# A decoder trunk on one core: attention's bias laid out per query by DMA, and attention's scale and shift in two halves

## The chip, the core and the metric

The kernel runs on one core of one Trainium2 chip. The metric is the device time of one execution in microseconds (us), as the median of the runs; lower is better. The profile is that of one more execution, recorded by the hardware profiler.

## The reference

Two decoder layers on 256 tokens of width 1024, all in fp32. Layer 0 has a pooling mixer and a dense SwiGLU; layer 1 has differential attention with a bias that depends on the distance of query and key, and then a mixture of eight SwiGLU experts. Each sub-layer takes `rms_norm(x) * (1 + scale) + shift`, where scale and shift come from a conditioning vector `c`:

```python
mod_all = silu(c) @ w_mod + b_mod                    # shift, scale, gate, twice for each layer
h = rms_norm(x, norm_g[1, 0]) * (1 + scale1) + shift1
q, k, v = split(h @ w_qkv)
bias = rel_bias[rel_bucket(q_pos, k_pos)]            # depends on q_pos - k_pos alone
s = q @ k.T + bias[head]                             # for each of the 2 halves of a head
p = softmax(where(k_pos <= q_pos, s, -inf))
a = p[0] - lam * p[1]
x = x + gate1 * rms_norm((rms_norm(a @ v) * (1 - lambda_init)) @ w_o)
```

## The kernel before

All five engines run hand-ordered instruction streams that meet at semaphores. Weights come in units of 1 MB (two DMAs of 512 KB on SyncE's queue) into a ring of six, `raw`; a unit's slot is filled again when VectorE's `unit_done` says that the unit six before has been used. A weight unit is split into a high and a low part: ScalarE's `high` (L721, 1.9 us) copies it, rounded, into one of three slots of `whi`, VectorE's `low` (L1099, 2.3 us) subtracts and writes `wlo`. TensorE then does three products, high by high, low by high and high by low (`three`, L1665 to L1667). Units of `w_mod` are instead multiplied by columns of `silu(c)` on VectorE (L1111, L1113).

The change lies between the dense SwiGLU of layer 0 and attention. The order of the work there, for the two tiles `t` of 128 tokens:

- TensorE ends the down projection (tile 0, then tile 1). ScalarE squares each tile (`square_down`, L844), GpSimd makes the inverse root (L605, L607), VectorE gates it (`gated_tile`, L1161) and adds the residual (`residual_tile`, L1168). ScalarE squares the sum (`square_residual`, L849), GpSimd makes its inverse root, VectorE scales (`normalize_tile`, L1303), and TensorE turns the tile by eight transposes (L1881).
- TensorE also sums the rows of attention's scale and shift into columns: `column_sums`, L1870 and L1871, 16 products with one column, 32 records in the trace, at helper line L1683. VectorE makes `modc` of them (L1312, L1313), in its order behind `gated_tile` of tile 1 and ahead of `residual_tile` of tile 1.
- ScalarE's `modulate_tile(t, b)` scales and shifts half a turned tile, four instructions at L833, and rounds it (L836, `thi`); VectorE subtracts (`low_from`, L1103, `tlo`). ScalarE begins with this only after `square_residual(1)`. The first products of attention are the values' first half ("group 0"): tile 0 and then tile 1, each by two units of four blocks (`kh`), 12 products of 512 columns for each. Then come groups 1 to 5.

The bias: GpSimd stores a row of 384 values for each of 8 heads (L622, 12 KB, near 41 us) and reads it back with overlapping rows (L641, 1 MB, near 82 us), which gives each query its keys, but in reverse order of the queries. TensorE multiplies it by a reversed identity, four products of 512 columns in fp32 (`bias(b)`, L1874: 0 and 1 after the transposes of tile 0, 2 after those of tile 1, 3 after group 0), and ScalarE copies each result into `bias_t` (L866). VectorE's first `row_max` of attention waits for it (L1347).

## Time and profile before

| | us |
|---|---|
| median of 3 runs | 1382.52 (1381.74 to 1385.71) |
| the profiled execution | 1383.44 |
| its span in the trace | 1381.4 |

| engine | busy us | share |
|---|---|---|
| TensorE, products | 1348.3 | 98% |
| VectorE | 1163.2 | 84% |
| ScalarE | 900.8 | 65% |
| GpSimd | 76.6 | 6% |

A busy time says only that instructions were running, and TensorE's ends are modelled; what an edit is worth is read from the chain of waits at its place and from the timelines there. A product in fp32 gives two records. The granted clock of TensorE (PEclk) is 1.00 at 2.4 GHz and 0.50 at 1.2 GHz.

### The profile page before, as it was taken

What the parts mean: (1) busy time and instruction counts of PE and PEld (TensorE: products, weight loads), DVE (VectorE), ACT (ScalarE), POOL (GpSimd) and SP (SyncE); (2) the same over time, 40 slices, a digit from 0 to 9 for tenths busy, and PEclk for the clock granted to TensorE, in tenths of its full rate; (3) what the DMA queues carried; (4) which work ended last, traced back from release to release, by engine and by line L of the source; (5) the groups of instructions that cost most, each with busy time, mean ns of one, the idle gap of its engine ahead of it and who ended that gap; (6) DMA issues with size and microseconds to landing.
All of it is one profiled execution on the core that took longest, in us unless ns stands there. A gap on an engine that the chain in (4) does not pass through costs nothing.

```text
span 1381.4 us, 19455 instructions
## 1 busy us (share of the span) xinstructions
PE 1348.3 (98%) x6869; PEld 1124.0 (81%) x6869; DVE 1163.2 (84%) x944; ACT 900.8 (65%) x749; POOL 76.6 (6%) x95
## 2 busy tenths in 40 slices
PE   6999999999899999999999999999999999999996
PEld 4599999898678888888888888888888888888885
DVE  6867778788869988888888888888888888898884
ACT  3353334556657777777777777777777777777772
POOL 2610000100210000000000000000000000000000
PEclk9999999999999999999999999999999999999998
DMA  9998889688259999999999999999999999999990
GB/s 363 407 351 291 309 313 336 229 295 315 108 191 353 412 395 357 394 374 384 367 388 389 350 404 372 371 378 382 388 347 403 381 365 382 379 385 356 411 351 33
DMA packets 210074, 475.13 MB, mean 344 GB/s; under 512 B 14977, under 2 KB 38609, under 8 KB 210017
## 3 DMA queue, kind: packets, MB, share of 16 engines
q1 hardware_dynamic: 204928, 457.76, 88.6%
q0 software_dynamic: 4944, 16.35, 3.8%
q8 instruction: 35, 0.57, 0.2%
q10 hardware_dynamic: 144, 0.26, 0.0%
q14 instruction: 23, 0.18, 0.0%
HBM read 465.39 MB, written 8.93 MB: 343 GB/s over the span
## 4 chain that ended last, share of the span: by engine, by line
PE 93%; DVE 3%; ACT 1%; issue 1%; DMA 1%; POOL 0%; SPq 0%; DVEq 0%
PE ps L1665 29%; PE ps L1667 28%; PE ps L1666 28%; PE ps L2114 2%; DMA raw<-w_mod 1%; PE ps L1683 1%; DVE wlo L1443 1%; PE ps L1745 1%; PE ps L1949 0%; PE ps L2080 0%; PE ps L1649 0%; PE ps L1679 0%; DVE wlx L1443 0%; DVE hs L1392 0%; PE ps L2038 0%
## 5 line engine op out<-in xcount | busy, mean ns | idle before, releaser
L1443 DVE TENSOR_TENSOR wlx<-raw,whx 128x2048 fp32r<-128x2048 f32 x168 | 384.7, 2291 | 97.6 <-ACT whx L979 96.8
L1443 DVE TENSOR_TENSOR wlo<-raw,whi 128x2048 fp32r<-128x2048 f32 x168 | 384.0, 2287 | 4.5 <-ACT whi L979 3.0
L979 ACT ACTIVATE whi<-raw 128x2048 fp32r<-128x2048 f32 x168 | 322.3, 1920 | 88.7 <-PE ps L1667 87.0
L979 ACT ACTIVATE whx<-raw 128x2048 fp32r<-128x2048 f32 x168 | 322.3, 1919 | 83.7 <-PE ps L1667 83.7
L1665 PE MATMUL ps<-whi,thi 128*128 128x512 f32 x516 | 207.8, 403 | 1.1 <-DVE tlo L1415 0.6
L1667 PE MATMUL ps<-whi,tlo 128*128 128x512 f32 x516 | 201.6, 391 | 0.0
L1666 PE MATMUL ps<-wlo,thi 128*128 128x512 f32 x516 | 201.3, 390 | 0.0
L1665 PE MATMUL ps<-whx,thi 128*128 128x512 f32 x460 | 179.9, 391 | 0.5 <-DVE tlo L1415 0.5
L1667 PE MATMUL ps<-whx,tlo 128*128 128x512 f32 x460 | 179.2, 390 | 0.0
L1666 PE MATMUL ps<-wlx,thi 128*128 128x512 f32 x452 | 175.9, 389 | 0.0
L1665 PE MATMUL ps<-thi,whi 128*128 128x256 f32 x480 | 136.3, 284 | 2.1 <-DVE tlo L1103 2.1
L1666 PE MATMUL ps<-tlo,whi 128*128 128x256 f32 x480 | 135.8, 283 | 0.0
L1667 PE MATMUL ps<-thi,wlo 128*128 128x256 f32 x480 | 135.8, 283 | 0.0
L1099 DVE TENSOR_TENSOR wlo<-raw,whi 128x2048 fp32r<-128x2048 f32 x44 | 99.8, 2288 | 37.4 <-ACT whi L721 37.4
L1665 PE MATMUL ps<-whi,ahi 128*128 128x512 f32 x300 | 118.1, 394 | 0.6 <-DVE alo L1103 0.6
L1667 PE MATMUL ps<-whi,alo 128*128 128x512 f32 x300 | 116.8, 389 | 0.0
L1666 PE MATMUL ps<-wlo,ahi 128*128 128x512 f32 x300 | 116.8, 389 | 0.0
L1665 PEld LDWEIGHTS ps<-whi,thi 128*128 128x128 f32 x516 | 97.0, 188 | 23.4 <-issue 2.8
L1667 PEld LDWEIGHTS ps<-whi,tlo 128*128 128x128 f32 x516 | 96.8, 188 | 21.1
L1666 PEld LDWEIGHTS ps<-wlo,thi 128*128 128x128 f32 x516 | 97.1, 188 | 18.5 <-issue 0.2
L721 ACT ACTIVATE whi<-raw 128x2048 fp32r<-128x2048 f32 x44 | 83.0, 1907 | 41.0 <-PE ps L1667 41.0
L1665 PEld LDWEIGHTS ps<-whx,thi 128*128 128x128 f32 x460 | 86.4, 188 | 20.9 <-issue 3.2
(283 smaller groups left out, 1908.8 us busy)
## 6 DMA issues: line engine op xcount, KB each, us to landing
raw<-moe_w_gu SPq DMA_DIRECT2D x448, 512.0 KB, 6.2
raw<-moe_w_down SPq DMA_DIRECT2D x224, 512.0 KB, 6.4
raw<-w_mod SPq DMA_DIRECT2D x88, 512.0 KB, 5.6
raw<-ffn_w_gu SPq DMA_DIRECT2D x44, 512.0 KB, 5.3
raw<-w_qkv SPq DMA_DIRECT2D x24, 512.0 KB, 5.2
raw<-ffn_w_down SPq DMA_DIRECT2D x22, 512.0 KB, 5.0
shift_w<-w_mod SPq DMA_DIRECT2D x8, 512.0 KB, 15.7
raw<-w_o SPq DMA_DIRECT2D x8, 512.0 KB, 5.8
```

The source lines that it names most:

```text
L721: act.activation(whi[:, q % SPL, :], raw[:, r % RAW, :], ACT.Copy).then_inc(hi_ready, 1)
L979: act.activation(m_hi[m % MRING], raw[:, r % RAW, :], ACT.Copy).then_inc(hi_ready, 1)
L1099: dve.tensor_tensor(wlo[:, q % SPL, :], raw[:, r % RAW, :], whi[:, q % SPL, :].bitcast(F32), ALU.subtract).then_inc(unit_done, 1)
L1443: dve.tensor_tensor(m_lo[m % MRING], raw[:, r % RAW, :], m_hi[m % MRING].bitcast(F32), ALU.subtract).then_inc(unit_done, 1)
L1665: pe.matmul(out, a_hi, b_hi, start=start, stop=False, skip_group_check=check)
L1666: pe.matmul(out, a_hi, b_lo, start=False, stop=False, skip_group_check=check)
L1667: return pe.matmul(out, a_lo, b_hi, start=False, stop=stop, skip_group_check=check)
L1683: mm = pe.matmul(out[:, k:k + 1], rows[:, ROW[l][g], k * P:k * P + P], ones[:, 0:1], start=True, stop=True)
L1745: mm = pe.matmul(ps[:, 4 + 2 * t + g // 2, (g % 2) * FC:(g % 2) * FC + FC], pooled_t[:, 2 * g + k, t * P:t * P + P], poolw[:, g, k, :], st ...
L2114: mm = pe.transpose(ps[:, 6, jj * P:jj * P + P], actf[:, jj * P:jj * P + P], ident)
```

## The change

The 384 values of each head are stored once for each of the 128 queries, by one DMA that repeats its source (8 partitions, 128 times, 12 KB each: 1.57 MB written). It is issued by GpSimd after `f_ahi` counts 3 (third step of the dense SwiGLU) instead of near 41 us. The load goes straight into `bias_t`, with a step from query to query that is one value short of the stored row, so that the order is right; it is issued behind the last inverse root before attention. The reversed identity, its four products, ScalarE's four copies and the waits for them are gone. Scale and shift are summed in halves: `half_sums(0)`, the transposes of tile 0, then `half_sums(1)`, and four small products (`keep_clock`). `modc` follows in halves, the first ahead of `gated_tile` of tile 1, the second behind it. ScalarE modulates the first half of tile 0 ahead of `square_residual(1)`. The low part of the values' second unit is made in halves around VectorE's `normalize_tile(1)`, and the transposes of tile 1 move between the first and second half of group 0's tile 0.

```diff
-    consts[:, 4] = np.eye(P)[::-1]
...
-    bias_dram = nc.dram_tensor("bias_by_distance", (NH, S + P), F32, kind="Internal").ap()
+    bias_dram = nc.dram_tensor("bias_by_distance", (P, NH, S + P), F32, kind="Internal").ap()
...
-        bias_rev = scr[:, 4096:6144].rearrange("p (h k) -> p h k", h=NH)
...
-            pool.wait_ge(dist_ready, 2)
-            pool.dma_start(bias_dram, bias_row).then_inc(dist_stored, 16)
+            pool.dma_start(numbers[:, 0:3], consts_in[:, 4 * P:4 * P + 3]).then_inc(wr_loaded, 16)
+
             inverse_roots(0, 2)
             inverse_roots(1, 0)
...
             next_gain(3, (0, 2))
-            pool.dma_start(consts[:, 2:5, :], consts_in[:, 2 * P:5 * P].rearrange("p (i s) -> p i s", i=3)).then_inc(more_consts_loaded, 16)
-
+            pool.dma_start(consts[:, 2:4, :], consts_in[:, 2 * P:4 * P].rearrange("p (i s) -> p i s", i=2)).then_inc(more_consts_loaded, 16)
+
+
+            pool.wait_ge(dist_ready, 2)
+            pool.wait_ge(f_ahi, 3)
+            pool.dma_start(bias_dram.rearrange("q h k -> h q k"),
+                           bias_row.unsqueeze(1).broadcast_to([NH, P, S + P])).then_inc(dist_stored, 16)
             pool.wait_ge(dist_stored, 16)
-            pool.wait_ge(lam_prod, 2)
-            pool.dma_start(bias_rev, bass.AP(tensor=bias_dram.tensor, offset=0,
-                                             ap=[(1, P), (S + P, NH), (1, S)])).then_inc(bias_loaded, 16)
             next_gain(5, (0, 5))
             inverse_roots(1, 2)
             inverse_roots(2, 0)
+
+            pool.dma_start(bias_t, bass.AP(tensor=bias_dram.tensor, offset=P - 1,
+                                           ap=[(NH * (S + P) - 1, P), (S + P, NH), (1, S)])).then_inc(bias_loaded, 16)
 
...
@@ -853,17 +853,15 @@
             square_residual(0)
             square_down(1)
             high(R_QKV + 1, Q_QKV + 1)
+            act.wait_ge(col_ready, 7)
+            modulate_tile(0, 0)
             square_residual(1)
-            act.wait_ge(col_ready, 7)
-            for t in range(T):
-                for b in range(2):
-                    modulate_tile(t, b)
+            act.wait_ge(col_ready, 9)
+            modulate_tile(0, 1)
+            modulate_tile(1, 0)
+            modulate_tile(1, 1)
             act.wait_ge(ss_ready, 4 * 2 + T)
             high(R_GROUP[1], Q_QKV + 2)
-
-            def copy_bias(b):
-                act.wait_ge(bias_ps, b + 1)
-                act.copy(bias_t[:, 2 * b:2 * b + 2, :], bank(b).rearrange("p (h k) -> p h k", h=2)).then_inc(bias_ready, 1)
 
             def qkv_out(g):
                 act.wait_ge(unit_used, Q_QKV + 2 * g + 2)
@@ -875,11 +873,8 @@
                     dst = vs[:, :, (c - 4) * 512:(c - 3) * 512]
                 act.copy(dst, src).then_inc(qkv_ready, 1)
 
-            for b in range(3):
-                copy_bias(b)
             high(R_GROUP[1] + 1, Q_QKV + 3)
             qkv_out(0)
-            copy_bias(3)
             for g in range(2, 6):
                 high(R_GROUP[g], Q_QKV + 2 * g)
                 high(R_GROUP[g] + 1, Q_QKV + 2 * g + 1)
@@ -1306,20 +1301,37 @@
...
             gated_tile(0, 5, 0, Y1[0])
             residual_tile(0, T, Y1[0])
             normalize_tile(0)
+
+            def attention_columns(h):
+
+                a, b = slice(4 * h, 4 * h + 4), 3 - h
+                dve.wait_ge(col_ps, 6 + h)
+                dve.scalar_tensor_tensor(modc[:, 0, a], ps[:, b, 0:4], 1.0, cols[:, 8, a], ALU.add, ALU.mult).then_inc(col_ready, 1)
+                dve.tensor_copy(modc[:, 1, a], ps[:, b, 4:8]).then_inc(col_ready, 1)
+
+            attention_columns(0)
             gated_tile(0, 5, 1, Y1[1])
-
-            dve.wait_ge(col_ps, 7)
-            dve.scalar_tensor_tensor(modc[:, 0, :], ps[:, 3, 0:KC], 1.0, cols[:, 8, :], ALU.add, ALU.mult).then_inc(col_ready, 1)
-            dve.tensor_copy(modc[:, 1, :], ps[:, 3, KC:2 * KC]).then_inc(col_ready, 1)
+            attention_columns(1)
             residual_tile(1, T, Y1[1])
+
+            def low_tile(t, b):
+                dve.wait_ge(ht_hi, 4 + 2 * t + b + 1)
+                part = (slice(None), slice(4 * b, 4 * b + 4), slice(t * P, t * P + P))
+                low_from(tlo3[part], hv3[part], thi3[part], ht_lo)
+
+            def low_half(h, sem_out):
+
+                a, sl = slice(h * D, h * D + D), (Q_QKV + 1) % SPL
+                dve.wait_ge(hi_ready, Q_QKV + 2)
+                dve.tensor_tensor(wlo[:, sl, a], raw[:, (R_QKV + 1) % RAW, a], whi[:, sl, a].bitcast(F32), ALU.subtract).then_inc(sem_out, 1)
+
+            low_tile(0, 0)
+            low_half(0, values_lo)
             normalize_tile(1)
-            for t in range(T):
-                for b in range(2):
-                    dve.wait_ge(ht_hi, 4 + 2 * t + b + 1)
-                    part = (slice(None), slice(4 * b, 4 * b + 4), slice(t * P, t * P + P))
-                    low_from(tlo3[part], hv3[part], thi3[part], ht_lo)
-                    if t == 0 and b == 0:
-                        low(R_QKV + 1, Q_QKV + 1)
+            low_tile(0, 1)
+            low_half(1, unit_done)
+            low_tile(1, 0)
+            low_tile(1, 1)
             n = N_QKV_MODS
             for g in range(6):
                 if g:
...
                 dve.wait_ge(sc_ps, h + 1)
                 if h == 0:
-                    dve.wait_ge(bias_ready, 4)
+                    dve.wait_ge(bias_loaded, 16)
...
             down_tile(1, last_hi, last_lo, Q_LAST_DOWN % SPL, True).then_inc(unit_used, 1)
 
             pe.wait_ge(row_done, done_rank(0, 5))
-            column_sums(1, 1, ps[:, 3, 0:KC])
-            column_sums(1, 0, ps[:, 3, KC:2 * KC])
-
-            def bias(b):
-                pe.matmul(bank(b), reverse, bias_rev[:, 2 * b:2 * b + 2, :].rearrange("p h k -> p (h k)"),
-                          start=True, stop=True).then_inc(bias_ps, 1)
+            def half_sums(h):
+
+                for i, g in enumerate((1, 0)):
+                    for k in range(4):
+                        mm = pe.matmul(ps[:, 3 - h, 4 * i + k:4 * i + k + 1], rows[:, ROW[1][g], (4 * h + k) * P:(4 * h + k) * P + P],
+                                       ones[:, 0:1], start=True, stop=True)
+                mm.then_inc(col_ps, 1)
+
+            half_sums(0)
 
             def turn_normalized(t):
                 pe.wait_ge(h_ready, 2 * T + t + 1)
@@ -1881,13 +1896,11 @@
                         mm = pe.transpose(ps[:, 4 + 2 * t + b, (k % 4) * P:(k % 4) * P + P], hs[:, t, k * P:k * P + P], ident)
                     mm.then_inc(ht_ps, 1)
 
-            pe.wait_ge(bias_loaded, 16)
             pe.wait_ge(more_consts_loaded, 16)
             turn_normalized(0)
-            bias(0)
-            bias(1)
-            turn_normalized(1)
-            bias(2)
+            half_sums(1)
+            pe.wait_ge(col_ready, 7)
+            keep_clock(3, 4)
 
             def qkv_group(g):
 
@@ -1908,22 +1921,25 @@
 
             for t in range(T):
                 for kh in range(2):
+                    if t == 0 and kh == 0:
+                        pe.wait_ge(unit_done, R_GROUP[0] + 1)
+                    elif t == 0:
+
+                        turn_normalized(1)
+                        pe.wait_ge(values_lo, 1)
                     pe.wait_ge(ht_lo, 4 + 2 * t + kh + 1)
-                    if t == 0:
-                        pe.wait_ge(unit_done, R_GROUP[0] + kh + 1)
                     q = Q_QKV + kh
                     for kk in range(4):
                         k, w = 4 * kh + kk, slice(kk * 512, kk * 512 + 512)
+                        if t == 0 and k == 6:
+                            pe.wait_ge(unit_done, R_GROUP[0] + 2)
                         mm = three(bank(4 + t), thi3[:, k, t * P:t * P + P], tlo3[:, k, t * P:t * P + P],
                                    whi[:, q % SPL, w], wlo[:, q % SPL, w], k == 0, k == KC - 1, False)
                     if t:
                         mm.then_inc(unit_used, 1)
-            pe.wait_ge(col_ready, 7)
-            bias(3)
             for g in range(1, 5):
                 qkv_group(g)
             pe.wait_ge(qkv_ready, 4)
-            pe.wait_ge(bias_ready, 4)
```

## Rows read from the trace of the kernel before

**Rows 1.** The page's first line: span of the profiled execution.

```profile
span 1381.4 us, 19455 instructions
```

**Rows 2.** What TensorE waited for, all the run; columns: us in total, times, longest.

```profile
PE ps L1881 <- DVE hs L1303: 0.3, 1, 0.3
```

**Rows 3.** The chain that ended last, in order of time, 265 to 287 us; columns: start, us, what.

```profile
265.21 3.65 PE ps L1683 x32
...
272.49 0.76 DVE hs L1303
...
273.30 1.09 PE ps L1881 x8
...
274.39 0.86 PE ps L1874 x2
...
275.25 0.23 PE ps L1665
...
286.15 0.86 PE ps L1874 x2
```

**Rows 4.** Timeline of TensorE (PE), 262 to 276 us; columns: start, us, engine, line, operation.

```profile
268.70 1.95 PE L1881 MATMUL ps<-consts,hs 128*128 128x128 f32 x8
...
270.44 2.54 PE L1874 MATMUL ps<-scr,consts 128*128 128x512 f32 x4
```

**Rows 5.** Timeline of ScalarE (ACT), 240 to 345 us.

```profile
266.26 1.90 ACT L721 ACTIVATE whi<-raw 128x2048 fp32r<-128x2048 f32 x1
...
270.34 1.06 ACT L849 ACTIVATE ysb<-xs 128x1024 f32<-128x1024 f32 x1 [2.19 <-DVE xs L1168]
...
271.40 1.48 ACT L833 ACTIVATE tmp<-ps,modc 128x128 f32<-128x128 f32 x4
...
272.91 0.63 ACT L836 ACTIVATE thi<-tmp 128x512 fp32r<-128x512 f32 x1
```

**Rows 6.** Timeline of VectorE (DVE), 240 to 345 us.

```profile
266.48 1.22 DVE L1161 TENSOR_TENSOR ysb<-ps,rows 128x1024 f32<-128x1024 f32 x1
...
269.04 1.28 DVE L1168 SCALAR_TENSOR_TENSOR xs<-ysb,rstd,xs 128x1024 f32<-128x1024 f32 x1
...
273.58 0.69 DVE L1103 TENSOR_TENSOR tlo<-tmp,thi 128x512 fp32r<-128x512 f32 x1 [0.34 <-ACT thi L836]
...
281.55 2.30 DVE L1099 TENSOR_TENSOR wlo<-raw,whi 128x2048 fp32r<-128x2048 f32 x1 [1.11 <-ACT whi L721]
```

**Rows 7.** Windows: each engine's busy time, granted TensorE clock (PEclk), DMA share, GB/s.

```profile
67.00:68.00 1.00, 1.00 (x11) 1.00 (x9) 0.96 (x3) 0.61 (x1) 1.00 (x2) 0.50 1.09 386
...
264.00:268.00 4.00, 4.00 (x34) 3.80 (x32) 1.88 (x2) 3.57 (x5) 1.58 (x4) 1.00 0.04 11
...
268.00:272.00 4.00, 4.00 (x18) 3.15 (x18) 1.43 (x3) 1.81 (x5) 0.34 (x2) 0.57 0.00 0
```

**Rows 8.** Timeline of TensorE, small operations near 19 and 65 us.

```profile
19.35 3.57 PE L1683 MATMUL ps<-consts,rows 128*128 128x1 f32 x16 [0.96 <-DVE rows L1184]
...
64.92 1.94 PE L1784 MATMUL ps<-consts,rows 1*128 1x1 f32 x16
...
66.79 0.91 PE L1679 MATMUL ps<-zeros 128*128 128x128 bf16 x8
```

**Rows 9.** Timelines of SyncE's queue, 60 to 150 us, and of ACT, 80 to 160 us.

```profile
114.94 3.12 SPq L453 DMA_DIRECT2D raw<-ffn_w_gu  x4
...
127.66 3.70 ACT L721 ACTIVATE whi<-raw 128x2048 fp32r<-128x2048 f32 x2
```

**Rows 10.** DMA issues of the whole run: KB each, us from issue to landing.

```profile
raw<-ffn_w_gu SPq DMA_DIRECT2D x44, 512.0 KB, 5.3
...
scr<-bias_by_distance POOLq DMA_DIRECT2D x1, 1024.0 KB, 9.3
...
bias_by_distance<-scr POOLq DMA_DIRECT2D x1, 12.0 KB, 5.4
```

**Rows 11.** DMA queues between 70 and 100 us: packets, MB, share of 16 engines.

```profile
q0 software_dynamic: 576, 1.79, 15.0%
```

More of the change, by code:

```diff
@@ L120, in shape_constants @@
 def shape_constants():
-    consts = np.zeros((P, 5, P), np.float32)
+    consts = np.zeros((P, 4, P), np.float32)
     consts[:, 0] = np.eye(P)
@@ L149, in shape_constants @@
     numbers = np.arange(1, 3 * P + 1, dtype=np.float32).reshape(3, P).T
-    return np.concatenate([consts.reshape(P, 5 * P), numbers], axis=1), pool.reshape(P, -1), onehot
+    return np.concatenate([consts.reshape(P, 4 * P), numbers], axis=1), pool.reshape(P, -1), onehot
 def build_trunk(nc, x, c, w_mod, b_mod, norm_g, pool_w, pool_scale, w_qkv, w_o, subln_g, lambda_vecs,
@@ L187, in build_trunk @@
         tmp = sb("tmp", [P, 2304])
-        consts = sb("consts", [P, 5, P])
+        consts = sb("consts", [P, 4, P])
         subln = sb("subln", [P, 4])
@@ L212, in build_trunk @@
         modc = sb("modc", [P, 5, KC])
-        ident, ones, before, slots, reverse = (consts[:, i, :] for i in range(5))
+        ident, ones, before, slots = (consts[:, i, :] for i in range(4))
         thi3 = thi[:, :].rearrange("p (k s) -> p k s", k=KC)
@@ L371, in build_trunk @@
         bias_loaded = sem("bias_loaded")
-        bias_ps = sem("bias_ps")
-        bias_ready = sem("bias_ready")
         lam_prod = sem("lam_prod")
@@ L383, in build_trunk @@
         qkv_ready = sem("qkv_ready")
+        values_lo = sem("values_lo")
         sc_ps = sem("sc_ps")
@@ L618, in _ @@
             pool.dma_start(wr[:, :, :], w_router[0].rearrange("(k p) e -> p k e", p=P)).then_inc(wr_loaded, 16)
-            pool.dma_start(numbers[:, 0:3], consts_in[:, 5 * P:5 * P + 3]).then_inc(wr_loaded, 16)
-            pool.wait_ge(dist_ready, 2)
-            pool.dma_start(bias_dram, bias_row).then_inc(dist_stored, 16)
+            pool.dma_start(numbers[:, 0:3], consts_in[:, 4 * P:4 * P + 3]).then_inc(wr_loaded, 16)
             inverse_roots(0, 2)
```

## The prediction

> **What bounds the kernel now.** I read the page first, for the span [rows 1] and TensorE's 98% share, then what TensorE waited for. In the stretch that the change touches that list holds one entry, 0.3 us for the normalized tile 1 [rows 2]. So TensorE is never out of work for long there, and the question is which of its work between the down projection and attention's group 1 can go, and who is late once it has gone. The chain in order of time shows this: column sums from 265.21, then a piece through VectorE, ScalarE and GpSimd to `normalize_tile(1)` at 272.49, transposes at 273.30, `bias(2)` at 274.39, group 0 from 275.25 to 286.15 and `bias(3)` for 0.86 us [rows 3]. Group 1 starts at 287.01, and from there TensorE is solid for 45 us. My number is the new start of group 1, as what lies behind it moves with it: ScalarE, VectorE and the ring of weights are paced by TensorE there.
>
> **What goes.** Of the four bias products, 0 and 1 take 2.54 us at the low clock [rows 4]; but the chain at that time runs through the other engines to tile 1, so they fill a gap and are worth nothing by themselves. `bias(2)` and `bias(3)` are on the chain, 0.86 us each, 1.72 us together [rows 3]. ScalarE's four copies lie in waits for TensorE and are worth nothing. Group 0 must also no longer wait for the transposes of tile 1: it needs half a tile 0 alone.
>
> **The floor.** TensorE needs in any case 3.79 us of column sums (the 3.65 of the chain and its lead), 1.09 us for each set of transposes at the high clock, and 286.15 - 275.25 = 10.90 us for group 0 [rows 3]. From 265.05 that makes 265.05 + 3.79 + 2.18 + 10.90 = 281.9, and with a few tenths of small products some 282.3: at most 4.7 us could be gained. The rest of the working is why I expect little of it.
>
> **The new order, step by step.** A half of the sums is 16 records, half of 3.79, so 1.9 us: `half_sums(0)` runs from 265.05 to 266.95. VectorE, done with `normalize_tile(0)` at 266.5, waits for it and makes half of `modc` by 267.2; `gated_tile` of tile 1, 1.22 us, moves from 266.48 to 267.2 [rows 6], which nobody misses, because its residual has to wait anyway. The transposes of tile 0 follow from 267.0 to 268.1. ScalarE is free at 268.16, behind `high` [rows 5], and modulates the first quarter at once: 1.48 + 0.63 us, done at 270.3, where before it was done at 273.5.
>
> Then comes the new wait. VectorE's second half of `modc` waits for `half_sums(1)`, and queued behind it on VectorE stand the residual of tile 1, the low part that group 0 waits for, and everything after. At the high clock `half_sums(1)` ends at 270.0. At the low one 16 such records took 3.57 us near 19 us, against 1.9 [rows 8] (that stretch is shown with PEclk 1.00, but its products are twice as long as later ones, so I read it as the low clock). It then ends at 271.65. Which of the two? The granted clock was 1.00 from 264 to 268 and 0.57 from 268 to 272, behind 32 records of one column [rows 7]: the low level, 1.2 GHz, for most of that stretch. Near 64.9 us eight transposes and 16 narrow products (L1784) did not prevent a fall either: 0.50 at 67 to 68 [rows 7, 8]. The new order has just that mix there, so I take the fall, and 271.65. The Trainium skill ("TensorE: Matmul & The Clock Gate", HAM clock gate) says that the default state is throttled and activity releases the throttle. By that rule alone the new order, which puts less work on TensorE before group 0, has its first products at half speed; the trace agrees as far as the low clock at 268 to 272 goes.
>
> From 271.7 on: second half of `modc` 0.2 us, residual 1.28 [rows 6], to 273.1; low part 0.69 [rows 6], to 273.8. Group 0 then starts at 273.8, against 275.25: 1.45 us earlier. Its first 12 products take 10.90 / 4 = 2.73 us at the high clock and twice that at the low; I take three at the low clock, 0.6 us more, and end at 277.1. The transposes of tile 1 come now, 1.09 us, to 278.2. They need `normalize_tile(1)`: square of the residual at 273.15, and from there to the scaling 272.49 - 270.34 = 2.15 us as before [rows 3, 5], so 275.3 to 276.0, in time. Second half 278.2 to 280.9: its low weights come by halves, half of 2.30 us each [rows 6], the second at about 278.4, for the seventh product at 279.6, in time. Tile 1: ScalarE can modulate from 277.7, 2.1 us, and VectorE 0.69, so 280.5 and 282.6 for its two halves, against 280.9 and 283.6, in time. Group 0 ends at 286.35. Group 1 needs its low weights: `high` 281.9 to 283.8 and `low` 2.30 us to 286.15 [rows 5, 6], 0.2 us before they are wanted. **Sum:** 287.01 - 286.35 = 0.65 us. With the fall of the clock behind `half_sums(1)` instead of ahead of it, group 0 starts at 272.35, its first 12 products lose 1.3 us to the low clock, and the same addition gives 285.7, a gain of 1.3. I take the middle, **0.9 us**.
>
> **The DMAs.** Both are moved past work on GpSimd's queue. The load into `bias_t`, 1 MB, 9.3 us to land next to other traffic [rows 10], is issued near 275.5 and wanted after 330. The DMA share was 0.04 and 0.00 just before [rows 7], and the next unit is wanted by ScalarE 15 us later, so it costs nothing; without this cover it would be 2.7 us of all engines. It stands behind the last inverse root on GpSimd, and the next thing there is in attention. The store is new in kind. By the load's queue, 1.79 MB took 15.0% of 16 engines for 30 us, 72 engine-us [rows 11]; 1.57 MB are then 63, so 4 us on all 16 engines and 8 on 8. It is issued near 127.8. A weight unit issued at 114.94 lands 5.3 us later [rows 9, 10] and is read by the second `high` of the pair at 127.66, at 129.5: 9 us in hand. So I price it at nothing, with the ends: nothing (the old 1 MB load near 82 us also goes, without a gain, as TensorE didn't wait there), and the rival below. The 12 KB store took 5.4 us [rows 10], which is nearly all latency; 128 times that, 690 us, would be the far end and would block GpSimd past 256 us, where a gain is due. I don't believe it, since 0.5 to 32 KB all took about as long. One DMA that repeats a source has no row here.
>
> The rule that speaks against the store is in the Trainium skill ("DMA: Bandwidth & Descriptors", Rules for kernel authors): an outermost dimension below 16 confines a DMA to at most that many engines; here that is 8, heads being outermost. "SBUF — State Buffer" (Door 1) adds that four partitions share a port, at about 27 GB/s. By both, an estimate for 1.57 MB from 8 partitions is 29 us. No run here shows either yet.
>
> **Rivals.**
> 1. The clock stays up (`half_sums(1)` at 1.9 us and group 0 at full speed): group 0 starts at 272.35, and by the same steps group 1 at 284.4. Gain 2.6 us, 1379.9. For it: the clock is back at 1.00 right after 272; against it, the two falls above. 20%.
> 2. The low clock lasts through the whole first half of group 0: 12 products at twice 2.73 us, so 1.8 us beyond the forecast's 0.6, and group 1 at 288.2. That is the new wait on VectorE at its worst: a loss of 1.1 us, 1383.6. 12%.
> 3. The store starves the dense SwiGLU, **slower than before**. It decides once the engines that carry it are held for over 9 us. If they are held 16.6 us (half the 8 engines, or half the rate), the weights come 16.6 - 9.2 = 7.4 us late, less the 0.9 gained: 1389.0. For it: 8 source partitions only. Against it: other transfers keep their turns between its packets. 8%.
> 4. The floor: all waits vanish, and 4.7 us are gained, 1377.9. 5%.
> 5. The change doesn't do what it says, for one thing because group 1's low weights, 0.2 us in hand above, set its start again. This gives 1382 to 1383 and lies inside the forecast.
>
> **The numbers.** The profiled execution took 1383.44, its span 1381.4, so 2.0 us lie around it; it ran 0.9 above the median. The sum gives a span of 1380.5 and an execution of 1382.5; on the median's footing 1382.52 - 0.9 = 1381.6. The forecast, 0.3 to 1.6 us gained, has 55%. The range takes in rivals 1 and 2 and half a us of spread on each side: 1379.4 to 1384.2, with rivals 3 and 4 left out. 0.3% is 4.1 us, about what a measurement of this kernel can tell from no change: only rival 4 is faster by that, 5%; rival 3 slower, 8%; the rest is the same, 87%.
>
> **What would show it.** In the changed kernel: `half_sums(1)` at about 3.5 us with a granted clock of 0.5; group 0 starting some 1.5 us earlier counted from the first column sum, its first products 0.43 us apart at first; group 1 0.3 to 1.6 us earlier; no wait of TensorE for weights between 128 and 180 us; the store landing before 170 us. The prediction is wrong if TensorE waits in the dense SwiGLU, if group 1 starts over 2 us earlier or later than now, or if attention or the experts take another time than before.

## The result

The changed kernel is slower: median 1400.53 us of 4 runs (1397.42 to 1401.94), beside 1384.12 us (1381.74 to 1386.69) for the kernel before in 4 runs. The ratio is 1.0115, with an interval of 1.0099 to 1.0132. The forecast was 1381.6 in a range up to 1384.2, so the time lies 16 us above the top of the range, on the side that had 8%.

The profiled execution took 1400.59 us. The page of the changed kernel begins as follows; the span line answers to [rows 1], and the third line names what stands in the chain that ended last.

```profile
span 1398.7 us, 19447 instructions
...
PE 91%; DVE 4%; DMA 3%; ACT 1%; issue 1%; SPq 0%; DVEq 0%; POOL 0%; ACTq 0%
PE ps L1677 28%; PE ps L1679 27%; PE ps L1678 27%; DMA raw<-ffn_w_gu 2%; PE ps L2130 2%; PE ps L1768 1%; DMA raw<-w_mod 1%; PE ps L1757 1%; DVE wlo L1094 0%; PE ps L1965 0%; DVE wlo L1455 0%; PE ps L2096 0%; ACT whi L721 0%; PE ps L1695 0%; PE ps L1691 0%
```

The span grew by 17.3 us. The entry to look at is `raw<-ffn_w_gu`: 2% of 1399 us, a load of weights of the dense SwiGLU on the chain. What TensorE waited for between 100 and 340 us says it directly (us in total, times, longest):

```profile
PE ps L1677 <- DVE wlo L1094: 13.9, 2, 13.5
PE ps L1677 <- DVE tlo L1098: 2.0, 1, 2.0
```

Before, this list held one entry of 0.3 us in the same stretch [rows 2]. The second line is the start of attention's group 0, to which I come below. For the first, the chain in order of time leads back to its source, 140 to 172 us:

```profile
142.12 0.84 SPq L450
142.96 0.04 issue
143.00 26.45 DMA raw<-ffn_w_gu
169.45 0.02 issue
169.48 1.92 ACT whi L721
171.40 0.02 issue
171.42 2.31 DVE wlo L1094
```

A load of 512 KB, half a unit, was on its way for 26.45 us; such loads took 5.3 us before [rows 10]. The timelines of GpSimd, ScalarE and TensorE give the order of events: the store is issued, ScalarE waits for weights, TensorE runs out and then starts again with slow products.

```profile
129.81 1.13 POOL L637 DMA_DIRECT2D bias_by_distance<-scr  x1 [46.47 <-ACT ahi L813]
...
166.76 1.91 ACT L721 ACTIVATE whi<-raw 128x2048 fp32r<-128x2048 f32 x1 [18.88 <-DMA raw<-ffn_w_gu]
...
171.05 0.58 PE L1677 MATMUL ps<-thi,whi 128*128 128x256 f32 x1 [13.54 <-DVE wlo L1094]
```

And the DMA issues of the stretch, the view of [rows 10]: KB each, median us from issue to landing.

```profile
raw<-ffn_w_gu SPq DMA_DIRECT2D x4, 512.0 KB, 25.9
raw<-w_mod SPq DMA_DIRECT2D x4, 512.0 KB, 7.8
bias_by_distance<-scr POOLq DMA_DIRECT2D x1, 1536.0 KB, 35.2
```

The store, issued at 129.8, lands at 165.0. Within 1.8 us of it ScalarE has its unit, and 6.0 us after it TensorE works again. The windows of the changed kernel show the same as a rate (columns: stretch, sum, busy us of PE, PEld, DVE, ACT and POOL with their counts, PEclk, DMA share, GB/s):

```profile
140.00:148.00 8.00, 8.00 (x67) 7.92 (x66) 6.01 (x7) 3.04 (x3) 0.00 (x0) 1.00 0.68 106
148.00:156.00 8.00, 8.00 (x53) 7.28 (x52) 2.21 (x1) 0.00 (x0) 0.00 (x0) 1.00 0.50 58
156.00:164.00 8.00, 1.51 (x7) 0.93 (x5) 0.00 (x0) 0.00 (x0) 0.00 (x0) 0.80 0.60 91
164.00:172.00 8.00, 0.95 (x4) 0.95 (x5) 2.87 (x2) 4.30 (x3) 0.00 (x0) 0.50 0.99 371
```

In the kernel before, the last three of these stretches were

```profile
148.00:156.00 8.00, 8.00 (x48) 7.04 (x46) 6.22 (x4) 2.26 (x2) 0.00 (x0) 1.00 0.77 247
156.00:164.00 8.00, 8.00 (x68) 8.00 (x67) 6.01 (x7) 3.52 (x4) 0.00 (x0) 1.00 1.01 358
164.00:172.00 8.00, 8.00 (x51) 7.23 (x50) 6.32 (x3) 3.23 (x2) 0.00 (x0) 1.00 0.77 252
```

A DMA share of 0.50 beside 58 GB/s is the sign to learn: half of the DMA engines' time is taken, and what they move is about a quarter of what they moved before (58 beside 247 GB/s, then 91 beside 358). Much time and few bytes means that each byte takes long. Why it does is what the experiments ask.

**Where the 17.3 us went.** Up to the first column sum, my landmark, the distance grew by 282.31 - 265.05 = 17.26 us, and behind it the rest of the span is 1116.39 against 1116.35. So all of it lies ahead. 13.54 us are the wait. Behind it the first 16 products come 0.21 us apart and not 0.12 (PEclk is 0.50 until 174), which costs 1.5 us. A second wait of 0.40 us stands at 184.67. 1.35 us lie ahead of the dense SwiGLU, whose first product starts at 76.89 and not 75.54. Together this is 16.8; half a us is spread too thinly to be named. The 1.35 us are not the change's: kernels with the same code up to there differ by more. The kernel before starts it at 75.54, and at 77.10 with small products added far behind; the four kernels below whose store reads 128 partitions start it between 73.59 and 76.93.

### The profile page after: what moved, and what is told of

Read it like the earlier page. It is cut to its first block, busy times and chain, and to the rows that moved or that the text cites. A ratio compares the mean times of both kernels' runs of the same rounds, so it can differ in the third digit from the quotient of the medians.

```text
span 1398.7 us, 19447 instructions
## 1 busy us (share of the span) xinstructions
PE 1350.6 (97%) x6865; PEld 1126.9 (81%) x6865; DVE 1163.5 (83%) x947; ACT 899.5 (64%) x745; POOL 79.3 (6%) x95
## 4 chain that ended last, share of the span: by engine, by line
PE 91%; DVE 4%; DMA 3%; ACT 1%; issue 1%; SPq 0%; DVEq 0%; POOL 0%; ACTq 0%
PE ps L1677 28%; PE ps L1679 27%; PE ps L1678 27%; DMA raw<-ffn_w_gu 2%; PE ps L2130 2%; PE ps L1768 1%; DMA raw<-w_mod 1%; PE ps L1757 1%; DVE wlo L1094 0%; PE ps L1965 0%; DVE wlo L1455 0%; PE ps L2096 0%; ACT whi L721 0%; PE ps L1695 0%; PE ps L1691 0%
## 5 line engine op out<-in xcount | busy, mean ns | idle before, releaser
L1677 PE MATMUL ps<-thi,whi 128*128 128x256 f32 x480 | 136.8, 285 | 15.6 <-DVE wlo L1094 13.5
L1677 PEld LDWEIGHTS ps<-thi,whi 128*128 128x128 f32 x480 | 92.8, 193 | 16.6 <-DVE wlo L1094 14.0
```

Of the source, the lines that this page charges most:

```text
L1677: pe.matmul(out, a_hi, b_hi, start=start, stop=False, skip_group_check=check)
```

## Experiments

A landing time is from issue to landing, and "group 1" is the time from the first column sum to the second product of attention's group 1 (the first is stretched in some traces). It is 21.92 us before and 21.05 in the changed kernel. The kernel before was timed beside each set of runs.

### One copy in place of 128

The bias is stored once, as before; the load has a step of +1, so that the 128 rows of a head come in reverse order (this kernel's bias, and so its output, is that of reversed queries). All else is the changed kernel.

```diff
-            pool.dma_start(bias_dram.rearrange("q h k -> h q k"),
-                           bias_row.unsqueeze(1).broadcast_to([NH, P, S + P])).then_inc(dist_stored, 16)
+            pool.dma_start(bias_dram, bias_row).then_inc(dist_stored, 16)
...
-            pool.dma_start(bias_t, bass.AP(tensor=bias_dram.tensor, offset=P - 1,
-                                           ap=[(NH * (S + P) - 1, P), (S + P, NH), (1, S)])).then_inc(bias_loaded, 16)
+            pool.dma_start(bias_t, bass.AP(tensor=bias_dram.tensor, offset=0,
+                                           ap=[(1, P), (S + P, NH), (1, S)])).then_inc(bias_loaded, 16)
```

> The changed kernel with the bias stored once (12 KB) at the same place instead of 128 times, and loaded with a step of one value, so that the queries of the bias come in reverse order: the output differs for that reason alone, the sizes of the load are the same. Theory A: TensorE has no wait for weights in the dense SwiGLU, and what is left is the gain of the columns and of the bias products: 0.5 to 1.5 us faster than the kernel before, with 20.9 us from the first column sum to group 1, as in the changed kernel, against 22.0 before. Rival B: it stays 10 us or more slower than before.

Measured: 1384.34 us against 1384.62, ratio 1.000 (0.9988 to 1.0012). The store landed in 3.8 us, and TensorE had no wait between 100 and 260 us. Group 1 came after 20.87 us. So the loss is the size or the shape of the store, and not the place of the step, the new order in attention, or the load. The gain of 0.5 to 1.5 us that I expected can't be seen in this ratio, nor does its interval rule it out.

### The store alone, in the kernel before

```diff
+    copies_dram = nc.dram_tensor("bias_copies", (P, NH, S + P), F32, kind="Internal").ap()
...
+            pool.wait_ge(bias_loaded, 16)
+            pool.wait_ge(f_ahi, 3)
+            pool.dma_start(copies_dram.rearrange("q h k -> h q k"),
+                           bias_row.unsqueeze(1).broadcast_to([NH, P, S + P])).then_inc(dist_stored, 16)
+            pool.wait_ge(dist_stored, 32)
             next_gain(5, (0, 5))
```

> The kernel before, with one addition: the 128-fold store of 1.57 MB from partitions 0 to 7, into a DRAM tensor that nobody reads, issued by GpSimd once the third step of the dense SwiGLU is through, as in the changed kernel. Theory A (the store alone makes the loss): it lands after about 35 us, TensorE waits some 13 us for low weights near 170 us, and the time is 14 to 17 us above the kernel before. Rival B (the store is slow, but the loss needs the rest of the change): within 3 us of the kernel before.

Measured: 1400.63 us against 1383.45, ratio 1.0126 (1.0103 to 1.0148). Its DMA issues and the waits of TensorE between 100 and 340 us:

```profile
bias_copies<-scr POOLq DMA_DIRECT2D x1, 1536.0 KB, 35.1
...
PE ps L1671 <- DVE wlo L1105: 13.8, 2, 13.4
```

The same landing, the same wait, the same loss (17.2 us, at the edge of the 14 to 17 expected). This one DMA, which nobody reads, makes the kernel before as slow as the changed one. The pair is complete: without the store the loss is gone, and with the store alone it is there.

### Which property of the store costs it

The bytes, 1.57 MB, stay; what changes is which partitions they are read from. In the first kernel the product that looks the bias up writes it to all 128 partitions (its table of 8 columns is repeated 16 times by the DMA that loads it), and the store reads partitions 0, 9, 18 and so on to 63, 8 of them as before, 128 times each. In the second it reads partitions 0 to 15, 64 times each.

```diff
-            pool.dma_start(relb, rel_bias).then_inc(small_loaded, 16)
+            pool.dma_start(relb.rearrange("b (r h) -> b r h", h=NH),
+                           rel_bias.unsqueeze(1).broadcast_to([N_BUCKETS, P // NH, NH])).then_inc(small_loaded, 16)
...
+            pool.dma_start(bass.AP(tensor=bias_dram.tensor, offset=0,
+                                   ap=[(S + P, 8), (8 * (S + P), 128), (1, S + P)]),
+                           bias_row[0:64:9, :].unsqueeze(1).broadcast_to([8, 128, S + P])).then_inc(dist_stored, 16)
```

> The changed kernel, the same store of 8 rows, 128 times each, but with the row of head h taken from partition 9h (0, 9, ..., 63) instead of partition h. For that the rows are made on all 128 partitions by the same product, with the table's 8 columns repeated 16 times. Theory P (the source's partitions share few ports, two for partitions 0 to 7, eight here): the store lands in 10 to 15 us instead of 35, and the time falls by 12 us or more. Theory E (8 engines carry it, because the outermost dimension is 8, and each is slow by itself): 35 us as before and 1400 us.

```diff
+            pool.dma_start(bass.AP(tensor=bias_dram.tensor, offset=0,
+                                   ap=[(S + P, 16), (16 * (S + P), 64), (1, S + P)]),
+                           bias_row[0:16, :].unsqueeze(1).broadcast_to([16, 64, S + P])).then_inc(dist_stored, 16)
```

> The changed kernel with the store's source on 16 partitions (0 to 15), 64 times each, so an outermost dimension of 16. Theory P (four ports): the store lands after about 20 us. Theory E (16 engines instead of 8): about 20 us as well. Both expect most of the wait of TensorE in the dense SwiGLU gone, 0 to 5 us left of 13.5; read with the run that keeps 8 rows on spread partitions it tells ports from engines.

A third reads all 128 partitions, 8 times each. Here ScalarE repeats the table on the chip, so that the start of the kernel isn't held up:

```diff
+            act.copy(relb_wide.rearrange("b (r h) -> b r h", h=NH),
+                     relb.unsqueeze(1).broadcast_to([N_BUCKETS, P // NH, NH])).then_inc(relb_spread, 1)
...
+            pool.dma_start(bass.AP(tensor=bias_dram.tensor, offset=0,
+                                   ap=[(S + P, 128), (128 * (S + P), 8), (1, S + P)]),
+                           bias_row[0:128, :].unsqueeze(1).broadcast_to([128, 8, S + P])).then_inc(dist_stored, 16)
```

> The changed kernel with the store's source on all 128 partitions, 8 times each: the rows are made for 16 copies of the heads by one product, whose table ScalarE widens by a copy. Theory P (the ports of the source's partitions set the rate; 2 ports took 35.2 us, 4 took 18.5, 8 took 12.3): 16 ports leave only the engines' own time, so it lands in 7 to 10 us, no wait of TensorE for weights. Theory E (only the number of engines counts): with 16 engines like the source of 16 partitions, 18 us. Time: the kernel before less 0 to 1.5 us.

The DMA queues of the changed kernel, 130 to 166 us, and its store; then those of the 8 partitions nine apart, 130 to 150 us (packets, MB, share of 16 engines):

```profile
q0 software_dynamic: 704, 1.58, 43.2%
q1 hardware_dynamic: 1846, 2.63, 22.1%
```

```profile
q1 hardware_dynamic: 2858, 4.81, 69.1%
q0 software_dynamic: 704, 1.58, 22.7%
...
bias_by_distance<-scr POOLq DMA_DIRECT2D x1, 1536.0 KB, 12.3
```

Both stores have 8 source partitions, 704 packets and 1.58 MB in these windows. The first holds engines for 0.432 x 16 x 36 = 249 engine-us, the second for 0.227 x 16 x 20 = 73. Meanwhile the queue of weights moves 2.63 MB in 36 us in the one and 4.81 MB in 20 us in the other. The others by the same sum:

| source partitions | lands in us | engine-us | wait of TensorE for weights, us |
|---|---|---|---|
| 8 side by side (changed kernel) | 35.2 | 249 | 13.5 |
| 16 side by side | 18.5 | 0.577 x 16 x 25 = 231 | 1.6 |
| 8, nine apart | 12.3 | 73 | none |
| 128 | 11.9 | 0.194 x 16 x 22 = 68 | none |

So the number of source partitions isn't it (8 give 73 or 249), nor the bytes, nor the destination, which is the same in that pair. With 8 or 16 partitions side by side, the time per byte on an engine is 3 to 4 times as long as in the other two rows. The store from 16 lands sooner than that from 8 at nearly the same engine-us: on average it holds 231 / 18.5 = 12.5 engines at once, against 249 / 35.2 = 7.1. Both the partitions and the outermost dimension were doubled, so this step doesn't tell which of the two helped. The two stores from 8 partitions do: they differ only in how far apart the partitions lie.

The packets of the weights were hardly slower themselves: 0.221 x 16 x 36 = 127 engine-us for 2.63 MB, 48 for each MB, against 0.691 x 16 x 20 = 221 for 4.81 MB, 46 for each, next to the store from partitions nine apart. The weights were late because of the time between their packets, which fits engines that are busy with the store. Which of the 16 engines the store held stays open.

The Trainium skill ("SBUF — State Buffer", Door 1) says that four neighbouring partitions share a port and gives some 27 GB/s for each. By that, the four stores read through 2, 4, 8 and 16 ports, at 54, 108, 216 and 435 GB/s, and with the 5.4 us of the small store [rows 10] for the rest they should land in 34.5, 20.0, 12.7 and 9.0 us, an estimate. The traces agree for the first three: 35.2, 18.5 and 12.3. The fourth took 11.9 us here, with 6.57 MB of weights in the same 22 us, more than this estimate and than the 7 to 10 us expected; in the three later kernels with the same store it took 10.5, 7.9 and 7.8. Its sister rule, at most 8 engines for an outermost dimension of 8 ("DMA: Bandwidth & Descriptors", Rules for kernel authors), is not what makes the difference of the pair: the stores from 8 partitions nine apart and from 8 neighbours are alike in it.

Two of these kernels have a single time each: 1387.8 us (nine apart) and 1388.41 us (16). Their repeated table landed late, and TensorE started some 3.5 us later, with `[3.76 <-DMA scr<-onehot_in]` in its timeline at 14.55; that is this experiment's way of preparing the table, and no verdict on the store. The kernel with 128 source partitions has no such wait: 1383.58 us against 1383.45, ratio 1.0004 (0.999 to 1.0018). The change as it stands, with its source spread over the partitions, costs nothing and brings nothing that can be measured.

The same can be had without SBUF as a source. The row is stored once, early, and a second DMA makes the 128 copies from DRAM to DRAM, queries outermost:

```diff
+            pool.wait_ge(dist_ready, 2)
+            pool.dma_start(bias_once, bias_row).then_inc(dist_stored, 16)
...
+            pool.wait_ge(f_ahi, 3)
+            pool.dma_start(bias_dram, bias_once.unsqueeze(0).broadcast_to([P, NH, S + P])).then_inc(dist_stored, 16)
+            pool.wait_ge(dist_stored, 32)
```

> The changed kernel, but the 12 KB row is stored to DRAM early, as in the kernel before, and the 128 copies are made by one DMA from DRAM to DRAM, queries outermost, so no SBUF port is read. Theory P (the source's SBUF ports made the 35 us): it lands in 7 to 13 us, TensorE does not wait for weights, and the time is that of the kernel before within 2 us. Rival W (the 1.57 MB of writes to DRAM, in pieces of 1.5 KB, are slow in themselves): 20 us or more.

Measured: the copies landed in 9.1 us and held 0.289 x 16 x 15 = 69 engine-us; no wait for weights. Its single time is 1381.07 us; its dense SwiGLU began at 73.52, 2.0 us earlier than before, so this one time proves no gain. But it speaks against slow writes to DRAM as the cause: the same bytes were written here.

### The order of attention, and its clock

My forecast let the clock fall ahead of group 0, and rival 1 let it stay up. First the order alone, on top of the store from 128 partitions: the residual of tile 1 goes ahead of the second half of the columns on VectorE, so that it waits for no product.

```diff
             gated_tile(0, 5, 1, Y1[1])
-            attention_columns(1)
             residual_tile(1, T, Y1[1])
+            attention_columns(1)
```

> As the run with the source on 128 partitions, and on VectorE the residual of tile 1 stands ahead of the second half of modc, so that it doesn't wait for the second half of the column sums. If that wait is what holds up group 0, group 0 starts 0.6 to 1.3 us earlier, counted from the first column sum (about 5.7 to 6.3 us instead of 6.7 to 7.0), and group 1 0.3 to 1.2 us earlier (19.7 to 20.6 instead of 20.8 to 20.9). If ScalarE's modulation sets it, group 0 starts at the same time and nothing moves. The whole time may move by less than can be told.

Measured: 1385.11 us against 1383.45, ratio 1.0013 (1.0002 to 1.0024), so no gain, and if anything 0.1% lost. Its group 0 starts 6.04 us after the first column sum (7.1 with the store from 128 partitions alone), but group 1 comes after 20.51 us, only 0.35 earlier than there. TensorE's windows of 2 us, from 4.0 us behind the first column sum on, say why:

```profile
267.10:269.10 2.00, 0.91 (x8) 0.64 (x8) 1.58 (x5) 1.97 (x4) 0.00 (x0) 0.57 0.00 0
269.10:271.10 2.00, 1.97 (x5) 1.63 (x6) 1.23 (x2) 1.97 (x7) 1.63 (x3) 0.50 0.00 0
271.10:273.10 2.00, 2.00 (x6) 1.54 (x5) 2.00 (x3) 0.25 (x1) 1.02 (x1) 0.50 0.16 16
```

Group 0 is earlier, and its first half runs at 1.2 GHz. In the stretch ahead of it TensorE was busy for 0.91 of 2 us.

Now the same kernel with small products of zeros (128x128, bf16) in the gaps, which need no data of their own and are thrown away:

```diff
             half_sums(0)
+            keep_clock(0, 8)
...
             half_sums(1)
-            pe.wait_ge(col_ready, 7)
-            keep_clock(3, 4)
+            keep_clock(0, 24)
```

> As the run with the residual first, and with more small products on TensorE: 8 behind the first half of the column sums and 24 behind the second half, in place of 4. If the low clock that group 0's first products ran at in the changed kernel (0.50 from 288 to 292 us, products 0.43 us apart instead of 0.23) comes from too little work ahead of them, the clock stays at 1.00, and group 1 starts up to 2 us earlier than in the run with the residual first: 18 to 19.5 us from the first column sum. If the clock falls all the same, the small products cost up to 1 us in its place.

Measured: 1379.64 us against 1383.45, ratio 0.9974 (0.9962 to 0.9986). Its windows, from the first column sum on, and TensorE's timeline there:

```profile
264.90:266.90 2.00, 2.00 (x23) 1.98 (x22) 0.86 (x3) 1.78 (x3) 1.17 (x4) 1.00 0.00 0
266.90:268.90 2.00, 2.00 (x24) 2.00 (x21) 1.89 (x4) 2.00 (x4) 0.29 (x1) 1.00 0.03 8
268.90:270.90 2.00, 2.00 (x31) 2.00 (x32) 1.67 (x5) 1.97 (x4) 0.00 (x0) 1.00 0.00 0
270.90:272.90 2.00, 2.00 (x14) 1.66 (x12) 1.24 (x2) 1.97 (x7) 1.60 (x3) 1.00 0.00 0
```

```profile
267.94 1.84 PE L1893 MATMUL ps<-consts,rows 128*128 128x1 f32 x16
269.65 1.50 PE L1697 MATMUL ps<-zeros 128*128 128x128 bf16 x24
270.96 0.48 PE L1683 MATMUL ps<-whi,thi 128*128 128x512 f32 x1
```

The clock stays at 1.00 all through, group 0 starts 6.04 us after the first column sum, exactly as without the small products, and group 1 comes after 18.16 us: 3.76 less than before, where the median shows 3.8. So these 24 small products delay nothing, as group 0 can't start before its operands are there, and they bring the clock.

How much of it is the order, and how much the clock? With the small products, but VectorE's order as in the change:

> As the run named warm, but with the order of VectorE as in the changed kernel (the second half of modc ahead of the residual of tile 1): it tells what the small products give without the other edit. In the traces so far the residual first brought group 0 1.1 us earlier and group 1 0.35 us, at the low clock. If the clock is the larger part, group 1 starts 18 to 19.5 us from the first column sum, and the time is 2 to 4 us below the kernel before. If the small products pay only together with the earlier residual, since group 0 otherwise starts so late that the clock falls, group 1 starts at 20 us or later, and the time is that of the kernel before.

Measured: 1381.11 us against 1384.10, ratio 0.998 (0.9969 to 0.999); group 1 after 19.18 us. The clock thus brings 20.86 - 19.18 = 1.7 us, and the order 19.18 - 18.16 = 1.0 us at the high clock. At the low one it brought 0.35: most of the earlier start was lost to more products at half speed (products 2 to 12 of group 0 came 0.43 us apart on average, and 0.37 with the later start).

And the small products without the change, in the kernel before:

```diff
             column_sums(1, 1, ps[:, 3, 0:KC])
+            keep_clock(0, 8)
             column_sums(1, 0, ps[:, 3, KC:2 * KC])
+            keep_clock(0, 8)
```

> The kernel before with 8 small products between the two column sums and 8 behind them. The low clock there, 268 to 272 us, lies on transposes of tile 0 and on bias products 0 and 1, which fill a gap of the chain. If a low clock costs only where TensorE is on the chain, nothing is gained, and the first 8 products, which stand ahead of the sums that modc waits for, cost up to 0.5 us: group 1 22 us from the first column sum, as before or up to 0.5 later, and the time within 1.5 us of the kernel before. If the clock is worth something by itself, group 1 starts a us or more earlier.

Measured: 1384.55 us against 1384.10, ratio 1.0013 (1.0 to 1.0026): nothing gained, and group 1 after 22.26 us. TensorE's timeline of this kernel:

```profile
268.11 1.84 PE L1683 MATMUL ps<-consts,rows 128*128 128x1 f32 x16
269.81 0.61 PE L1679 MATMUL ps<-zeros 128*128 128x128 bf16 x8
270.25 1.90 PE L1683 MATMUL ps<-consts,rows 128*128 128x1 f32 x16
272.01 0.63 PE L1679 MATMUL ps<-zeros 128*128 128x128 bf16 x8
```

The second sum is delayed by the first eight, and the operands of what follows come through VectorE and ScalarE. The granted clock fell all the same, to 0.61 at 272 to 274 and 0.53 at 274 to 276. So this run does not show what a clock held at 1.00 would bring in the kernel before. There was little to win there: its first 12 products of group 0 came 0.23 us apart already, at full speed. Small products paid where a hole stood ahead of products on the chain, and the change is what made that hole.

Last, the copy from DRAM to DRAM with both edits of attention:

> The copies made from DRAM to DRAM as in the run of that name, with the small products (8 behind the first half of the column sums, 24 behind the second) and the residual of tile 1 first, as in the run named warm. It asks whether the gain of that run comes back under another form of the store. If it is the clock and VectorE's order, group 1 starts 18 to 18.5 us from the first column sum, and the time is 2.5 to 4.5 us below the kernel before. If that run was helped by the wide source or by chance, the time is within 1.5 us of the kernel before.

Measured: 1379.78 us against 1384.51, ratio 0.9971 (0.996 to 0.9982); group 1 after 18.17 us, clock 1.00. This and the kernel with 128 source partitions and the same two edits are one result, 4.7 and 3.8 us faster than before and some 21 faster than the change as it stands.

## The prediction, point by point

**The store: wrong, and it decides.** I priced it as 63 engine-us, "8 on 8" engines, from the load's queue [rows 11], with 9 us in hand, so at nothing. It held 249 engine-us, four times that, and landed after 35.2 us. The failed term is the 63. Its row was of a transfer that spread over 128 partitions, and I took from it a price per byte on an engine, as if that were the engine's own. For a source of that kind it was right: 73, 68 and 69 engine-us where the source was 8 partitions apart, 128 partitions, or DRAM. For 8 neighbours it wasn't. The estimate by the Trainium skill's two pages, 29 us for the bytes, stood beside the sum, and the measured 35.2 less 5.4 is 29.8. I kept it out of the sum, as no row showed it, but it should have raised the chance of rival 3: nothing in the trace spoke against it, since no row there had so few partitions with so many bytes. The one "against" that I gave, that other transfers keep their turns, gave no protection: whatever turns they had, the whole traffic was 58 GB/s.

**Rival 3: the right mechanism, at the wrong size.** The store starves the dense SwiGLU, as it said. It took the hold for 16.6 us, half the real one, and the cover for 9.2. The cover is longer: 18.5 us cost 1.6 us of waiting and 35.2 us cost 13.5, so 0.7 us for each further us, and by this line the first loss comes near 16 us (an estimate from two points, of stores that differ in how many engines they kept busy; 12.3 cost nothing). The two errors point in opposite directions; at its own 16.6 us the rival's 7.4 would have been near 0. What I also left out is that a stalled TensorE comes back at half speed, 1.5 us.

**Where the loss ends.** "The store landing before 170 us" was met, at 165.0, and the time was lost all the same. It was a badly chosen sign: what mattered was its distance from the last weights in hand, which ran out at 157.5. "No wait of TensorE for weights between 128 and 180 us" was the right one, and it fell.

**Group 1: right in its sum, wrong in its parts.** Forecast 0.9 us earlier, measured 21.92 - 21.05 = 0.87. The timeline of the changed kernel:

```profile
282.31 1.84 PE L1886 MATMUL ps<-consts,rows 128*128 128x1 f32 x16
...
284.92 1.84 PE L1886 MATMUL ps<-consts,rows 128*128 128x1 f32 x16
286.62 0.38 PE L1691 MATMUL ps<-zeros 128*128 128x128 bf16 x4
288.97 0.77 PE L1677 MATMUL ps<-whi,thi 128*128 128x512 f32 x1 [1.96 <-DVE tlo L1098]
```

`half_sums(1)` took 1.84 us and not the 3.57 that I chose by [rows 8]; the clock fell only behind it. Group 0 started 6.66 us after the first column sum, where I had 273.8 - 265.05 = 8.75, and before it was 9.64 (274.69 in the timeline; the 275.25 that I took from the chain is where `bias(2)` leaves it). But all of its first 12 products were slow, 0.43 us apart until 293.8, and I had three. These are the two ends that I had worked out: the fall behind `half_sums(1)`, and rival 2's low clock throughout the first half. I had them as cases apart, and they came together: group 0 2.1 us earlier than forecast, and more lost after it. That 0.87 lies so near to 0.9 is therefore luck. (Rival 2 is also mis-added by its own words: 12 products at twice 2.73 us are 2.1 us beyond the 0.6, not 1.8.) Nor does the clock always fall behind `half_sums(1)`: in the kernels with the small store, with 8 partitions nine apart and with 128, whose code is the same there, it took 2.09, 2.17 and 2.29 us. The new wait is where I put it, on VectorE's low part (1.96 us), with the residual of tile 1 queued behind the second half of the columns.

**What became of the 0.87 us.** It isn't seen in a median: without the store's cost, the ratios are 1.000 and 1.0004, whose intervals leave room for a gain of 1 us. In the profiled execution it was given back behind group 1, 0.74 us of it in the router, whose 16 narrow products were quick before and slow in the changed kernel:

```profile
402.85 1.95 PE L2038 MATMUL ps<-wr,scr 128*128 128x8 f32 x16 [0.24 <-ACT scr L964]
...
419.13 2.69 PE L2054 MATMUL ps<-wr,scr 128*128 128x8 f32 x16 [0.24 <-ACT scr L959]
```

In the kernel before with the store alone, where attention is untouched, they took 3.36 us, so I don't lay this on the change. They were slow too with the small store (3.08) and with 128 source partitions (3.33), the kernels with the ratios 1.000 and 1.0004, and quick (1.95) in both kernels with both edits of attention. Whether its earlier arrival moves the fall of the clock onto them, or chance does, wasn't settled.

**The rest.** Rival 1 (the clock stays up) didn't happen, and became true with the small products: its 2.6 us compare with 2.7 (19.18 against 21.92) for the change's own order. Rival 4, a gain of 4.7 us, is nearly reached by the two edits together, 3.76. Rival 5, that group 1's low weights set its start, didn't happen. The load of 1 MB landed 6.5 us after its issue at 290.64 and cost nothing, as forecast.

## What to carry to other kernels

Ask of a DMA not only how many bytes it moves, but through how many different partitions, and how far apart they lie: a source of a few neighbouring partitions repeated many times holds the DMA engines that other loads need. When an operation has no row of its kind in the trace, a price that only a page gives deserves a chance of its own, the size of what speaks for and against it, and not a place outside the sum. When work is taken from the engine on the chain, look at what the hole does to its clock, and fill the hole with products that need no data if what follows is on the chain.

## What the runs showed of the hardware

- A store of 1.57 MB from 8 neighbouring partitions took 35.2 us and 249 engine-us, from 8 partitions nine apart 12.3 us and 73. Next to the first, a load of 512 KB on another queue took 25.9 us in place of 5.3.
- Held engines show as a DMA share of 0.5 to 0.6 beside 58 to 91 GB/s. The share alone would have looked like spare room.
- 16 products of one column took 1.84 us with a granted clock of 1.00, and behind them it was 0.75, then 0.50, in the changed kernel, with 1.96 us of waiting in between. No wait is needed for the fall: in the kernel before it was 0.57 with TensorE busy throughout, behind 32 such records [rows 7]. With 8 and 24 products of 128 columns in the gaps it stayed at 1.00, in all three kernels that have them, and the 12 products behind came 0.23 us apart instead of 0.43.
- The packets of the weights took 48 engine-us for each MB next to the slow store and 46 next to a quick one: loads of 512 KB landed after 25.9 us in place of 5.3 though their own packets were hardly slower.
